# Mixture-of-experts positions of 96 + 32 rows on TensorE's column groups 64 + 32 + 32, and three experts loaded before routing

## What is computed

```python
def moe_ffn(h, w_router, router_bias, we_gate, we_up, we_down, ws_gate, ws_up, ws_down):
    ...
    scores = jax.nn.sigmoid(jnp.dot(t.astype(jnp.float32), w_router.astype(jnp.float32)))
    ...
    _, idx = lax.top_k(jnp.where(exp_mask, sel, -jnp.inf), TOP_K)
    ...
    out = (jax.nn.silu(t @ ws_gate) * (t @ ws_up)) @ ws_down
    for e in range(N_EXPERTS):
        hid = jax.nn.silu(t @ we_gate[e]) * (t @ we_up[e])
        out = out + gates[:, e:e + 1] * (hid @ we_down[e])
```

## Time and profile before

| | us |
|---|---|
| median of 3 runs | 707.49 (707.42 to 708.46) |
| the profiled execution | 708.67 |
| its span | 706.9 |
| TensorE busy, all of the span | 642.9 (91%) |
| VectorE, ScalarE, GpSimd busy | 293.1, 130.7, 43.4 |
| weights and other data moved | 250.72 MB |

### The profile page before, as it was taken

One profiled execution on the slowest core, in us unless ns is written; L12 is line 12 of the kernel. 1 busy time (PEld: TensorE's weight loads), 2 busy tenths in 40 slices (PEclk: granted clock), 3 DMA queues, 4 the chain that ended last, 5 costly groups with the idle time before them and its releaser, 6 DMA issues.

```text
span 706.9 us, 11349 instructions
## 1 busy us (share of the span) xinstructions
PE 642.9 (91%) x4206; PEld 374.9 (53%) x4206; DVE 293.1 (41%) x775; ACT 130.7 (18%) x278; POOL 43.4 (6%) x223
## 2 busy tenths in 40 slices
PE   0469999999998899999999999999999999997882
PEld 0448886854544555556545565455554555553440
DVE  4649996778274233231332313323233232331115
ACT  3501123031320111111111111111111111111112
POOL 7000000000201000000000000000000000000000
PEclk9999999999999999999999999999999999999997
DMA  7998699724029999999999999999999999999951
GB/s 232 395 386 313 246 353 373 292 108 178 1 86 424 420 421 421 419 421 420 420 421 418 423 420 420 422 420 422 420 419 420 420 420 420 421 420 420 420 228 61
DMA packets 46010, 250.72 MB, mean 355 GB/s; under 512 B 4673, under 2 KB 7809, under 8 KB 20993
## 3 DMA queue, kind: packets, MB, share of 16 engines
q1 hardware_dynamic: 44434, 248.59, 86.6%
q10 hardware_dynamic: 1520, 1.39, 0.6%
HBM read 248.91 MB, written 1.05 MB: 354 GB/s over the span
## 4 chain that ended last, share of the span: by engine, by line
PE 67%; DVE 17%; DMA 12%; issue 1%; ACT 1%; ACTq 1%; SPq 0%; DVEq 0%
PE PS L1529 10%; PE PS L1525 9%; PE PS L1535 9%; PE PS L1508 8%; DVE MOD L871 7%; DMA ring<-in_we_up_dram 7%; PE PS L1583 5%; DMA ring<-in_w_ada_dram 5%; PE PS L1561 5%; PE PS L1557 5%; PE PS L1566 4%; PE PS L1579 2%; PE PS L1544 2%; PE PS L1325 1%; PE PS L1471 1%
## 5 line engine op out<-in xcount | busy, mean ns | idle before, releaser
L1167 DVE SCALAR_TENSOR_TENSOR arena<-arena,gate,PS 128x128 f32<-128x128 f32 (+1 forms) x48 | 17.9, 373 | 176.6 <-ACT arena L786 176.6
L1529 PE MATMUL PS<-ring,arena 128*64 128x256 f32 x736 | 88.4, 391 | 0.0
L1325 PE MATMUL PS<-hT,ring 128*128 128x256 f32 x384 | 84.8, 380 | 0.0
L1325 PEld LDWEIGHTS PS<-hT,ring 128*128 128x128 f32 x384 | 72.5, 190 | 11.1 <-issue 1.6
L1178 DVE TENSOR_TENSOR YLO<-PS,YHI 128x512 fp32r<-128x512 f32 x57 | 39.4, 691 | 93.3 <-ACT YHI L797 93.3
L871 DVE SCALAR_TENSOR_TENSOR MOD<-ring,ccol,MOD 128x768 f32<-128x768 f32 (+2 forms) x72 | 66.9, 930 | 13.1 <-ACT MOD L664 6.7
L1535 PE MATMUL PS<-ring,arena 128*32 128x256 f32 x1024 | 64.4, 403 | 7.5 <-DMA ring<-in_we_up_dram 7.5
L1508 PE MATMUL PS<-G,H2HI 128*128 128x256 f32 (+1 forms) x256 | 69.5, 307 | 1.3 <-ACT arena L777 0.7
L1525 PE MATMUL PS<-ring,arena 128*128 128x512 f32 x144 | 66.4, 612 | 0.6 <-issue 0.6
L1529 PEld LDWEIGHTS PS<-ring,arena 128*64 128x64 f32 x736 | 49.6, 134 | 31.7 <-issue 2.1
L797 ACT CAST YHI<-PS 128x512 fp32r<-128x512 f32 x57 | 33.5, 587 | 169.3 <-PE PS L1561 79.7
(11 more groups left out here) (255 smaller groups left out, 623.5 us busy)
## 6 DMA issues: line engine op xcount, KB each, us to landing
ring<-in_we_gate_dram SPq DMA_DIRECT2D x64, 1024.0 KB, 18.1
ring<-in_we_up_dram SPq DMA_DIRECT2D x64, 1024.0 KB, 20.7
ring<-in_we_down_dram SPq DMA_DIRECT2D x64, 1024.0 KB, 19.3
ring<-in_w_ada_dram SPq DMA_DIRECT2D x5, 3072.0 KB, 11.4
ring<-in_w_in_dram SPq DMA_DIRECT2D x3, 3072.0 KB, 18.0
ring<-in_w_ada_dram SPq DMA_DIRECT2D x4, 1536.0 KB, 15.8
ring<-in_w_out_dram SPq DMA_DIRECT2D x1, 3072.0 KB, 18.7
ring<-in_w_ada_dram SPq DMA_DIRECT2D x1, 2048.0 KB, 26.0
```

The lines of the kernel that those rows point to most:

```text
L1325: mm = pe.matmul(PS[:, 2 + q % QB, 0:TOK], w[:, k, (m % 6) * P:(m % 6) * P + P], hT[:, k, :], start=(k == 0), stop=(k == KD - 1))
L1529: m = pe.matmul(PS[64 * c:64 * c + 64, 6, 0:FE].rearrange("p (a n) -> p a n", a=2), xt[:, k, :], gu_cols(w[0], k, c), start=(k == 0), stop ...
```

## The change

- A new kind of position, mixed: one expert of up to 96 rows and one of up to 32. In `gate_up` and in each half of `down` it has three matmuls where a wide one has one: rows 0 to 63 and 64 to 95 with the first expert's weights, rows 96 to 127 with the second's.
- 2 wide, 9 mixed, 22 narrow positions and 11 pairs: 44 positions in 15 units. The first unit has two positions, wide and mixed, so all four gathers of the second unit come in one place.
- Experts 0, 1 and 2 are fixed; 1 and 2 are the first experts of mixed positions 1 and 2. Expert 3 is the second of position 1, expert 4 that of position 2.
- `sort_experts` works out the room of an expert in three steps in place of two. GpSimd makes the table `slotsm` of mixed positions.
- `onehot` has room for five experts of a unit and lies in another place.

```diff
-FIXED = 1
-WIDE, NARROW, PAIR = "wide", "narrow", "pair"
-UNITS = ([[WIDE, PAIR, NARROW]]
-         + 4 * [[PAIR, NARROW, WIDE], [NARROW, PAIR, WIDE], [NARROW, PAIR, NARROW]]
-         + 3 * [[NARROW, PAIR, NARROW]])
+FIXED = 3
+WIDE, MIXED, NARROW, PAIR = "wide", "mixed", "narrow", "pair"
+UNITS = [[WIDE, MIXED],
+         [MIXED, PAIR, NARROW],
+         [NARROW, NARROW, WIDE],
+         [PAIR, NARROW, MIXED],
+         [NARROW, PAIR, NARROW],
...
+         [NARROW, PAIR, NARROW]]
...
-ROWS = {WIDE: 128, NARROW: 64, PAIR: 32}
+ROWS = {WIDE: [128], MIXED: [96, 32], NARROW: [64], PAIR: [32, 32]}
...
+fixed, ranked = list(range(FIXED)), list(range(FIXED, NE))
+for kind in KIND:
+    first = [fixed.pop(0)] if fixed and kind in (WIDE, MIXED) else []
+    EXPERTS.append(first + [ranked.pop(0) for _ in ROWS[kind][len(first):]])
...
-            return 2 if KIND[p] == WIDE else 1
+            return 2 if KIND[p] in (WIDE, MIXED) else 1
...
+                link(pool.iota(slotsm[:, sub, :], pattern=[[1, P]], base=-96 * sub, channel_multiplier=0,
+                               allow_small_or_imprecise_dtypes=True))
+                link(pool.memset(slotsm[:, sub, 96 * (1 - sub):128 - 32 * sub], -1000.0))
...
-                link(dve.tensor_scalar(more, rank, NWIDE - 0.5, 64.0, ALU.is_lt, ALU.mult))
-                link(dve.tensor_tensor(cap, more, capcol[0:NE, :], ALU.add))
-                link(dve.tensor_scalar(more, rank, NWIDE + NNARROW - 0.5, 32.0, ALU.is_lt, ALU.mult))
-                link(dve.tensor_tensor(cap, cap, more, ALU.add))
+                for n, rows in enumerate((96, 64, 32)):
+                    link(dve.tensor_scalar(more, rank, N_OVER[rows] - 0.5, 32.0, ALU.is_lt, ALU.mult))
+                    link(dve.tensor_tensor(cap, more, cap if n else capcol[0:NE, :], ALU.add))
...
+                    elif KIND[p] == MIXED:
+                        for r0, r1, u in ((0, 64, 0), (64, 96, 0), (96, 128, 1)):
+                            m = pe.matmul(PS[r0:r1, 6, :].rearrange("p (a c n) -> p a c n", a=2, c=FT),
+                                          xt[:, k, r0:r1], gu_cols(w[u], k), start=(k == 0), stop=(k == KD - 1))
...
+                    elif KIND[p] == MIXED:
+                        for r0, r1, u in ((0, 64, 0), (64, 96, 0), (96, 128, 1)):
+                            m = pe.matmul(PS[r0:r1, 5, :], HTT[:, p % 2, cc * P + r0:cc * P + r1],
+                                          w[u][:, cc, 512 * half:512 * half + 512], start=(cc == 0),
+                                          stop=(cc == FT - 1))
...
-                if p and not (KIND[p] == WIDE and KIND[p - 1] != WIDE):
+                if p and not halves(p) > halves(p - 1):
                     add_up(p - 1)
```

More of the change, by code:

```diff
@@ L51 @@
 GU = 2 * KD * FE
-FIXED = 1
-WIDE, NARROW, PAIR = "wide", "narrow", "pair"
-UNITS = ([[WIDE, PAIR, NARROW]]
-         + 4 * [[PAIR, NARROW, WIDE], [NARROW, PAIR, WIDE], [NARROW, PAIR, NARROW]]
-         + 3 * [[NARROW, PAIR, NARROW]])
+FIXED = 3
[5 more added lines that the diff above has]
+         [NARROW, PAIR, NARROW],
+         [PAIR, NARROW, MIXED],
+         [NARROW, NARROW, MIXED],
+         [PAIR, NARROW, MIXED],
+         [NARROW, PAIR, NARROW],
+         [PAIR, NARROW, MIXED],
+         [NARROW, NARROW, MIXED],
+         [PAIR, NARROW, MIXED],
+         [NARROW, PAIR, NARROW],
+         [NARROW, PAIR, NARROW],
+         [NARROW, PAIR, NARROW]]
 KIND = [kind for unit in UNITS for kind in unit]
@@ L60 @@
 FIRST_POS = [UNIT_OF.index(i) for i in range(len(UNITS))]
-N_EXP = {WIDE: 1, NARROW: 1, PAIR: 2}
-ROWS = {WIDE: 128, NARROW: 64, PAIR: 32}
+ROWS = {WIDE: [128], MIXED: [96, 32], NARROW: [64], PAIR: [32, 32]}
 EXPERTS = []
[L64 to L69, removed]
+fixed, ranked = list(range(FIXED)), list(range(FIXED, NE))
+for kind in KIND:
+    first = [fixed.pop(0)] if fixed and kind in (WIDE, MIXED) else []
+    EXPERTS.append(first + [ranked.pop(0) for _ in ROWS[kind][len(first):]])
 PROC = [q for qs in EXPERTS for q in qs]
@@ L75 @@
     USE.append(USE[PROC[q - NSLOT]] + 1)
[L76 to L80, removed]
+ROWS_OF = [ROWS[KIND[p]][EXPERTS[p].index(q)] for q, p in enumerate(POS_OF)]
+N_ROWS = {rows: ROWS_OF[FIXED:].count(rows) for rows in (128, 96, 64, 32)}
+N_OVER = {rows: sum(n for more, n in N_ROWS.items() if more > rows) for rows in N_ROWS}
+RANK = [N_OVER[ROWS_OF[q]] + ROWS_OF[FIXED:q].count(ROWS_OF[q]) for q in range(FIXED, NE)]
+MAXE = max(len([q for p in range(NPOS) if UNIT_OF[p] == i for q in EXPERTS[p]]) for i in range(len(UNITS)))
 NCOL = 4
@@ L150, in build @@
         slotsp = WR[:, 0:4, :].rearrange("p (s k) n -> p s (k n)", s=2)
+        slotsm = WR[:, 4:8, :].rearrange("p (s k) n -> p s (k n)", s=2)
         COL = sb("COL", [P, R_END])
@@ L163, in build @@
         RT = sb("RT", [P, TT, NE, NCOL], BF16)
-        rcur = sb("rcur", [P, TT, 4])
-        rtcur = sb("rtcur", [P, TT, 4, NCOL], BF16)
+        rcur = sb("rcur", [P, TT, MAXE])
+        rtcur = sb("rtcur", [P, TT, MAXE, NCOL], BF16)
         tokf = sb("tokf", [P, NPOS])
@@ L410, in parts_before @@
         def parts_before(p):
-            return sum(2 if kind == WIDE else 1 for kind in KIND[:p])
+            return sum(2 if kind in (WIDE, MIXED) else 1 for kind in KIND[:p])
         def unit_cols(i):
@@ L418, in unit_cols @@
                 for q in EXPERTS[p]:
-                    where[q] = (first, first + ROWS[KIND[p]])
-                    first += ROWS[KIND[p]]
+                    where[q] = (first, first + ROWS_OF[q])
+                    first += ROWS_OF[q]
             return where, first
@@ L601, in _ @@
             link(pool.memset(capcol[:], 32.0))
-            link(pool.memset(capcol[0:FIXED, :], 128.0))
+            link(pool.memset(capcol[0:FIXED, :], float(ROWS_OF[FIXED - 1])))
+            link(pool.memset(capcol[0:1, :], float(ROWS_OF[0])))
             link(pool.iota(idcol[:], pattern=[[0, 1]], base=1, channel_multiplier=1,
@@ L809, in _ @@
                     copy_hidT(p + 1)
-                if KIND[p] == WIDE:
+                if halves(p) == 2:
                     y_high(p, 1)
@@ L1115, in one_hots @@
                     p = POS_OF[q]
-                    row = {WIDE: slots[:], NARROW: slotsn[:], PAIR: slotsp[:, q - EXPERTS[p][0], :]}[KIND[p]]
+                    sub = EXPERTS[p].index(q)
+                    row = {WIDE: slots[:], MIXED: slotsm[:, sub, :], NARROW: slotsn[:],
+                           PAIR: slotsp[:, sub, :]}[KIND[p]]
                     for t in range(TT):
@@ L1643, in _ @@
                 down(p, 0)
-                if p and KIND[p] == WIDE and KIND[p - 1] != WIDE:
+                if p and halves(p) > halves(p - 1):
                     add_up(p - 1)
```

2 lines of the change are left out of this document (1 added, 1 removed).

## The result

The changed kernel takes **803.0 us** (median of 4 runs, 802.8 to 803.4) against 707.5 before (4 runs, 707.4 to 708.5): a ratio of 1.1347, 95% interval 1.1327 to 1.1367. The direction was foretold, the size was not: the forecast was 714.1 and the range ended at 722. What came is rival 1, whose time was 798.

The account below looks back on a forecast made before the run. The weight loads (DMA) were taken to bind: 15.0 us saved against about 22 idle gave +6.9, small terms -0.3, so +6.6 on the median of 707.49, 714.1 us; range 708.5 to 722.

Parts of the forecast that it names:

- rival 1: Mixed gate and down: the 64 group and the two 32 take turns, gate 16 us, +12.8 per position, about 798; chance 0.16.
- Is a mixed gate packed?: Mixed gate: whether 64 and 32 column groups run side by side; packing taken as likelier, 798 us if not.
- the term of 7.35 us for a mixed gate: Gates of mixed positions 1 and 2: 7.35 us each, taken between 7.20 and 7.52 if packing works.
- 5.1 us for both halves of down: Down of positions 0 and 1: both halves with transposes and the wait for YLO, 5.1 us each position.
- The weights bind: Expert stage: weight loads at 420 GB/s set the time; TensorE waits 7.5 us for the last two long loads.
- The sum for the stream: Loads after routing: down of expert 6 issued at 261.1, about 22 us idle, last pair's load about 679, +6.9 us.
- The two fixed experts: Experts 1 and 2 load before routing for free, taking 6 transfers, 15.0 us, off the stream, but they take slots.
- The -21 us of TensorE: Positions 48 to 44, units 16 to 15: -21 us of TensorE work, which buys nothing as TensorE waits for loads.
- Rival 3's threshold: Down of expert 6 issued at 254.2 breaks even, each us earlier gains one; saving whole gives 693; chance 0.05.
- 7 us quicker: First two positions: TensorE would need this for down of expert 6 to break even, though their gates alone are 14.4.
- such a loss for a pair's gate: Pair's gate after waits of 4.5 and 3.0 us: 5.23 and 5.44 instead of 3.76; stays in TensorE's slack.

Follow-up runs that it names:

- run 1: Changed kernel with mixed positions as four column groups of 32 in gate and down, in place of 64 + 32 + 32; 715.52 us, ratio 1.0103 to the kernel before.
- run 5: Changed kernel with four column groups of 32 and one fixed expert instead of three, units as in the change; 715.31 us, ratio 1.0109 to the kernel before.
- run 8: Changed kernel with four groups of 32, one fixed expert, units reordered with light positions behind the first mixed one; 707.49 us, ratio 0.9993 to the kernel before.
- run 6: Changed kernel with four groups of 32, three fixed experts, units reordered with light positions behind the first mixed one; 703.08 us, ratio 0.9918 to the kernel before.
- run 2: Changed kernel with each mixed gate doing all eight k on the 64 group first, then on the two of 32, down unchanged; 787.03 us, one run.

## Why the prediction was wrong

- **The step that failed** is the answer to "Is a mixed gate packed?", "I take packing as the likelier", and with it the term of 7.35 us for a mixed gate and 5.1 us for both halves of down. Measured: 16.52 us, and 3.99 a half. The argument was that groups overlap in narrow and pair positions. They do, but there all groups have one width, so those rows could not speak for two. The row that did bear on it, the 0.1 us more at a change of shape, was read as a price and not as a sign that two shapes follow one another. The unknown had two prices, 7.35 and about 16, and the range took in the first alone.
- **Rival 1** was right in mechanism and nearly in size. Its gate of 16 measured 16.52; its +12.8 for a mixed position measured (16.52 - 7.36) + 2 x (3.99 - 1.91) = +13.3; nine times the 0.5 between them is 4.7, close to the 5 us from 798 to 803. It had drawn on two changes of width of 0.1 a k; they are 0.13 each. The Trainium skill's rule that changing the tiling mode drains TensorE (TensorEngine Tiling (Array Packing), Key Properties) is the rule by which rival 1 was told. The trace agrees in this: the groups of 32 start at 227.804, 0.540 us after the last record of the 64, where two records of the 32 are 0.475 apart and their groups 0.007. The Trainium skill's other rule in the same place, that tiles operate independently, holds for groups of one width (starts 0.007 us apart) and not across widths.
- **"The weights bind"** was right for the kernel before, and stays so in run 1, where TensorE waits 22.5 us. In the changed kernel it no longer holds, since 9 x 13.3 = 120 us more work is far more than TensorE had to spare.
- **The sum for the stream** holds wherever packing does. Expert 4's gate at 216.14 (216 to 217), down of expert 6 at 261.06 (261.1), 21.7 us idle (22), the rate whole from 265 us on, the last pair's load landed at 679.6 (679):

```profile
654.94 24.69 DMA ring<-in_we_up_dram
...
679.77 5.42 PE PS L1554 x64
```

  This is run 1's chain; 714.8 us scaled to the kernel before of the prediction, against 714.1.
- **The two fixed experts** were called free, at the price of slots. That is right as far as runs 1 and 5 show: with the change's order their 15.0 us vanish whole. The -21 us of TensorE bought nothing, as said: run 8 has it busy 624.8 us for 642.9 before, and the same time.
- **Rival 3's threshold** (down of expert 6 at 254.2 breaks even, each us earlier gains one) was of the right kind. At 242.86 it would give 11 us less; run 6 has 5.3 less. It supposed an empty queue, and here gate and up of expert 7 stand just ahead, issued at 241.38, with 5.0 us of data: 241.4 + 2.2 + 5.0 + 411.7 + 4.0 = 664.3, where the load landed at 666.7; the other 2.4 us stay open. The prediction held the threshold out of reach because TensorE would have to be "7 us quicker"; another order of the units brought it in reach, once the groups had one width.

## What to carry to other kernels

In all of these runs (float32, all 128 rows) a packing on column groups was a packing only among groups of one width: cut the wider group into pieces of the narrow one's width, though this adds matmuls (803.0 to 715.5 us here for two lines). Where a form has no row in the trace, the two hypotheses about it belong in the range with both their prices, above all when they stand 80 us apart and only one resource's slack of some 7 us hides the difference. And where loads wait for slots in a fixed order, count the work between the order's start and the slot that is queued last; transfers taken out ahead of that wait were worth nothing here (runs 1 and 5). With the heavy position moved behind it they were worth 4.4 of their 15.0 us (runs 6 and 8).

## What the runs showed of the hardware

- Column groups of 64 and of 32 overlapped nowhere in these runs: 2.065 us for a k of 64 + 32 + 32, 0.92 for four of 32 with the same data. Two groups of 32 alone take as long as four, and so does one of 64, half of the columns idle: a turn is 0.92 us in each case (14.66 / 16 in run 2).
- A change of width costs 0.13 us (run 2 against the change).
- After a wait of 2.9 us for a load the granted clock of the next stretch was 0.59, a mean of the two levels of 1.2 and 2.4 GHz, and the gate took 9.05 us in place of 7.36. These are run 1's stretches around it, and the chain there:

```profile
388.00:392.50 4.50, 1.63 (x17) 0.33 (x10) 0.93 (x2) 0.76 (x2) 0.94 (x5) 1.00 1.01 419
392.50:396.50 4.00, 4.00 (x24) 1.34 (x28) 0.00 (x0) 0.00 (x0) 0.00 (x0) 0.59 1.02 424
```
```profile
392.50 9.05 PE PS L1544 x64
```

  So this wait of TensorE cost 1.7 us more than itself, hidden here since the loads stayed at 420 GB/s and TensorE waited for them again later. The prediction had such a loss for a pair's gate (5.23 and 5.44 for 3.76) and gave no cause; these rows show the lower clock behind it.
